# A two-layer trunk on one core: layer loops written out, an output stage of its own for the last layer, and 64 bytes more in one small tensor

## The reference, cut to what matters

```python
for l in range(2):
    h = h + 0.5 * swiglu(rmsnorm(h, ffn1_norm[l]), ffn1_w_in[l], ffn1_w_out[l])   # 1024 -> 2*2816 -> 1024
    u = rmsnorm(h, mix_norm[l]); parts = u @ w_in[l]
    y_a, y_b, y_c = sparse attention, pooling mixer, attention into 256 memory tokens
    h = h + (sum_i sigmoid(gate_i) * (y_i @ w_branch_i)) @ w_out[l]
    h = h + 0.5 * swiglu(rmsnorm(h, ffn2_norm[l]), ffn2_w_in[l], ffn2_w_out[l])
return rmsnorm(h, final_norm)        # x * rsqrt(mean(x*x) + 1e-6) * gain
```

## Time and profile before

| | |
|---|---|
| timed runs, median | 2253.84 us |
| profiled execution | 2246.63 us, span 2244.8 us |
| PE busy | 2216.6 us, 99% of the span |
| DVE, ACT, POOL busy | 42%, 23%, 59% |
| granted TensorE clock, mean | 0.997 of 2.4 GHz |
| chain that ended last | PE 93%, DVE 4%, issue, ACT, DMA 1% each |

### The profile page before, as it was taken

One profiled execution on the slowest core, in us unless ns is written; L12 is line 12 of the kernel. 1 busy time (PEld: TensorE's weight loads), 2 busy tenths in 40 slices (PEclk: granted clock), 3 DMA queues, 4 the chain that ended last, 5 costly groups with the idle time before them and its releaser, 6 DMA issues.

```text
span 2244.8 us, 31758 instructions
## 1 busy us (share of the span) xinstructions
PE 2216.6 (99%) x10262; PEld 1805.1 (80%) x10262; DVE 953.5 (42%) x1716; ACT 523.6 (23%) x1013; POOL 1325.7 (59%) x884
## 2 busy tenths in 40 slices
PE   9999999999999999999999999999999999999996
PEld 6888888877788888888888888888778888888885
DVE  5331344578855433023333223536877453321334
ACT  3110112443553210001111101125445432100111
POOL 7666657644436665665766566584444376656653
PEclk9999999999999999999999999999999999999998
DMA  5243223222113222332333332232211132223222
GB/s 183 96 134 107 94 80 118 93 69 68 62 54 107 94 94 86 101 103 76 105 102 121 110 107 94 76 130 78 69 62 66 48 121 95 93 83 105 99 79 76
DMA packets 68219, 209.88 MB, mean 93 GB/s; under 512 B 7536, under 2 KB 10776, under 8 KB 67864
## 3 DMA queue, kind: packets, MB, share of 16 engines
q1 hardware_dynamic: 64128, 203.62, 27.7%
q10 hardware_dynamic: 3992, 5.00, 0.7%
HBM read 206.48 MB, written 3.68 MB: 94 GB/s over the span
## 4 chain that ended last, share of the span: by engine, by line
PE 93%; DVE 4%; issue 1%; ACT 1%; DMA 1%; POOL 0%; DVEq 0%; ACTq 0%; POOLq 0%; SPq 0%
PE bank L608 29%; PE bank L607 28%; PE bank L606 28%; PE obank L859 1%; PE sbank L804 1%; PE tbank L826 1%; DVE picks L1356 1%; DVE top L1354 1%; PE obank L617 0%; PE sbank L796 0%; PE sbank L779 0%; DMA h<-in_xT 0%; PE obank L843 0%; PE sbank L757 0%; PE sbank L810 0%
## 5 line engine op out<-in xcount | busy, mean ns | idle before, releaser
L541 POOL TENSOR_TENSOR wL<-raw,wH 128x1024 fp32r<-128x1024 f32 (+3 forms) x424 | 896.0, 2113 | 35.4
L538 POOL TENSOR_SCALAR wH<-raw 128x1024 fp32r<-128x1024 f32 (+3 forms) x424 | 397.4, 937 | 842.1 <-PE bank L608 820.1
L608 PE MATMUL bank<-u0L,wH 128*128 128x512 f32 x1376 | 542.1, 394 | 0.0
L607 PE MATMUL bank<-u0H,wL 128*128 128x512 f32 x1376 | 539.3, 392 | 0.0
L606 PE MATMUL bank<-u0H,wH 128*128 128x512 f32 x1376 | 536.1, 390 | 0.0
L607 PEld LDWEIGHTS bank<-u0H,wL 128*128 128x128 f32 x1376 | 258.3, 188 | 61.1 <-issue 1.0
L606 PEld LDWEIGHTS bank<-u0H,wH 128*128 128x128 f32 x1376 | 258.3, 188 | 58.4 <-issue 1.0
L608 PEld LDWEIGHTS bank<-u0L,wH 128*128 128x128 f32 x1376 | 258.7, 188 | 51.5
L606 PE MATMUL bank<-u1H,wH 128*128 128x512 f32 x704 | 293.2, 416 | 0.0
L608 PE MATMUL bank<-hidL,wH 128*128 128x512 f32 x704 | 277.4, 394 | 0.0
L607 PE MATMUL bank<-hidH,wL 128*128 128x512 f32 x704 | 276.0, 392 | 0.0
(11 more groups left out here) (189 smaller groups left out, 2177.8 us busy)
## 6 DMA issues: line engine op xcount, KB each, us to landing
raw<-in_wA SPq DMA_DIRECT2D x176, 512.0 KB, 3.2
raw<-in_wM SPq DMA_DIRECT2D x96, 512.0 KB, 3.3
raw<-in_wB SPq DMA_DIRECT2D x64, 384.0 KB, 3.0
raw<-in_wB SPq DMA_DIRECT2D x64, 320.0 KB, 2.9
raw<-in_wR SPq DMA_DIRECT2D x32, 256.0 KB, 2.5
mem<-in_memT SPq DMA_DIRECT2D x2, 1024.0 KB, 6.9
near_bias<-bias_rows ACTq DMA_DIRECT2D x2, 1024.0 KB, 6.4
outT<-gate_a SPq DMA_DIRECT2D x4, 512.0 KB, 2.7
```

The lines of the kernel that those rows point to most:

```text
L538: pool.tensor_scalar(wH[:, w, 0:cols], raw[:, slot, 0:cols], 1.0, 0.0, ALU.mult, ALU.add).then_inc(rounded, 1)
L541: pool.tensor_tensor(wL[:, w, 0:cols], raw[:, slot, 0:cols], wH[:, w, 0:cols].bitcast(F32), ALU.subtract).then_inc(split_done, 1)
L607: pe.matmul(dst, b, hi[:, k, :], start=False, stop=False)
L608: mm = pe.matmul(dst, a, lo[:, k, :], start=False, stop=last and i == len(tiles) - 1)
```

## The change

There are four parts.

1. `for l in range(L)` takes the place of the loop over layers on PE, ACT and DVE (not on POOL and SP). Values of waits become constants there, except inside the loops over j.
2. The last layer has a last stage of its own. u0H, u0L and the copy to `h` are gone for it. DVE adds the residual in the bank, ACT squares out of the bank, and of blocks 0 to 3 ACT also writes bank times gain to `h`; blocks 4 to 7 stay in their banks. Seven squares are added up in `ssq`; the eighth goes to `ta`, and PE adds it by a second product into the same bank.
3. The output rows 4 to 7 are made by DVE out of the banks, rows 2 and 3 by DVE from `h`, rows 0 and 1 by POOL from `h`. Each row is its own transfer of 256 KB, six issued by SP and two by ACT.
4. `eps` has 48 floats in place of 32. All that is allocated after it moves by 64 bytes: `sg` to byte 128768 (1006 x 128), `u0H` to 133120 (1040 x 128), `u0L`, `hidH`, `hidL`, `yH`, `yL` likewise to a multiple of 128. Nothing ahead of it moves.

```diff
+LAST_BY_VECTOR = (4, 5, 6, 7, 2, 3)
+LAST_BY_POOL = (0, 1)
...
-        eps = sb("eps", [P, LINE // 4])
+        eps = sb("eps", [P, LINE // 4 + LINE // 8])
...
-            with pe.Fori(0, L) as l:
+            for l in range(L):
...
-            pe.wait_ge(ssq_added, L * 24 + 8)
-            mean_square(over_d[:, :], ssq, L * 5 + 1)
+            pe.wait_ge(norm_taken, L * 5 + 1)
+            pe.wait_ge(ssq_added, L * 24 + 7)
+            pe.matmul(obank[:, :], over_d[:, :], ssq[:, :], start=True, stop=False)
+            pe.wait_ge(squared, L * 24 + 8)
+            pe.matmul(obank[:, :], over_d[:, :], ta[:, :], start=False, stop=True).then_inc(norm_mean, 1)
...
+                    act.preload_act_table_set("natural_log_exp_and_others")
+                    for k in range(KD):
+                        act.wait_ge(h_added, l * 24 + (16 + k + 1))
+                        if k >= 2 and k < KD - 1:
+                            act.wait_ge(ssq_added, l * 24 + (24 + k - 1))
+                        act.activation(sbank[k % 2][:, :] if k < KD - 1 else ta[:, :], bank[k % BANKS][:, :],
+                                       ACT.Square).then_inc(squared, 1)
+                        if k < 4:
+                            act.activation(h[:, k, :], bank[k % BANKS][:, :], ACT.Copy,
+                                           scale=gain(G_NEXT, k)).then_inc(evacuated, 1)
...
+            for n, k in enumerate(LAST_BY_POOL):
+                act.wait_ge(out_ready_pool, n + 1)
+                act.dma_start(out[:, k, :], gate_a[:, k, :]).then_inc(out_stored[k], 16)
...
+            for k in range(KD):
+                total = bank[k % BANKS][:, :]
+                dve.wait_ge(unit_used, unit_at(L - 1, U_FFN2 + 60 + 2 * k + 1))
+                dve.scalar_tensor_tensor(total, total, 0.5, h[:, k, :], ALU.mult, ALU.add).then_inc(h_added, 1)
+                if k < KD - 1:
+                    dve.wait_ge(squared, L * 24 + (k + 1))
+                    dve.wait_ge(ssq_added, L * 24 + k)
+                    dve.tensor_tensor(ssq[:, :], sbank[k % 2][:, :], ssq[:, :], ALU.add).then_inc(ssq_added, 1)
             inverse_rms(L * 5 + 1, rms[:, :])
-            for k in range(KD):
-                dve.scalar_tensor_tensor(gate_a[:, k, :], h[:, k, :], gain(G_NEXT, k), rms[:, :],
-                                         ALU.mult, ALU.mult).then_inc(out_ready, 1)
+            for k in LAST_BY_VECTOR:
+                if k >= 4:
+                    dve.scalar_tensor_tensor(gate_a[:, k, :], bank[k % BANKS][:, :], gain(G_NEXT, k), rms[:, :],
+                                             ALU.mult, ALU.mult).then_inc(out_ready, 1)
+                else:
+                    dve.tensor_tensor(gate_a[:, k, :], h[:, k, :], rms[:, :], ALU.mult).then_inc(out_ready, 1)
```

More of the change, by code:

```diff
@@ L417, in trunk @@
         out_ready = sem("out_ready")
-        out_stored = [sem(f"out_stored{s}") for s in range(4)]
+        out_stored = [sem(f"out_stored{k}") for k in range(KD)]
+        out_ready_pool = sem("out_ready_pool")
         vector_step = sem("vector_step")
@@ L429, in apart @@
         def apart(eng, *waits):
-            waits = [(s, eng.to_reg(value)) for s, value in waits]
+            waits = [(s, value if isinstance(value, int) else eng.to_reg(value)) for s, value in waits]
             eng.wait_ge(gain_loaded, 16)
@@ L519, in _ @@
             layer(L - 1)
[L521 to L525, removed]
+            for n, k in enumerate(LAST_BY_VECTOR):
+                sp.wait_ge(out_ready, n + 1)
+                sp.dma_start(out[:, k, :], gate_a[:, k, :]).then_inc(out_stored[k], 16)
+            for k in LAST_BY_VECTOR:
+                sp.wait_ge(out_stored[k], 16)
         @block.gpsimd
@@ L583, in _ @@
                 ffn_units(U_FFN2)
+            pool.wait_ge(norm_taken, L * 5 + 2)
+            for k in LAST_BY_POOL:
+                pool.tensor_tensor(gate_a[:, k, :], h[:, k, :], rms[:, :], ALU.mult).then_inc(out_ready_pool, 1)
         @block.tensor
@@ L986, in _ @@
                           ).then_inc(bias_repeated, 16)
-            with act.Fori(0, L) as l:
+            for l in range(L):
                 def ffn(chunk, hid_from, root_n, hi, g, n_from):
@@ L1188, in _ @@
                 ffn(C_FFN2, sum(HALF), 5, u0H, G_NEXT, 24)
-                last_half(C_FFN2, 24, G_NEXT, u0H)
+                if l < L - 1:
+                    last_half(C_FFN2, 24, G_NEXT, u0H)
+                else:
[9 more added lines that the diff above has]
+                                           scale=gain(G_NEXT, k)).then_inc(evacuated, 1)
                 own.restart()
             root(L * 5 + 1, rms[:, :])
+            for n, k in enumerate(LAST_BY_POOL):
+                act.wait_ge(out_ready_pool, n + 1)
+                act.dma_start(out[:, k, :], gate_a[:, k, :]).then_inc(out_stored[k], 16)
+            for k in LAST_BY_POOL:
+                act.wait_ge(out_stored[k], 16)
         @block.vector
@@ L1240, in _ @@
             own.restart()
-            with dve.Fori(0, L) as l:
+            for l in range(L):
                 def ffn(unit, chunk, hid_from, norm_n):
@@ L1574, in _ @@
                 ffn(U_FFN2, C_FFN2, sum(HALF), 5)
-                last_half(U_FFN2, 24, G_NEXT, u0H, u0L)
-            inverse_rms(L * 5 + 1, rms[:, :])
-            for k in range(KD):
-                dve.scalar_tensor_tensor(gate_a[:, k, :], h[:, k, :], gain(G_NEXT, k), rms[:, :],
-                                         ALU.mult, ALU.mult).then_inc(out_ready, 1)
+                if l < L - 1:
+                    last_half(U_FFN2, 24, G_NEXT, u0H, u0L)
+            own.restart()
+            for k in range(KD):
[6 more added lines that the diff above has]
+                    dve.tensor_tensor(ssq[:, :], sbank[k % 2][:, :], ssq[:, :], ALU.add).then_inc(ssq_added, 1)
+            inverse_rms(L * 5 + 1, rms[:, :])
+            for k in LAST_BY_VECTOR:
+                if k >= 4:
+                    dve.scalar_tensor_tensor(gate_a[:, k, :], bank[k % BANKS][:, :], gain(G_NEXT, k), rms[:, :],
+                                             ALU.mult, ALU.mult).then_inc(out_ready, 1)
+                else:
+                    dve.tensor_tensor(gate_a[:, k, :], h[:, k, :], rms[:, :], ALU.mult).then_inc(out_ready, 1)
 def tiles(w):
```

## The result

The changed kernel takes 2258.73 us (median of 10 runs, 2257.98 to 2259.55). The kernel before took 2254.11 us beside it (10 runs, 2246.24 to 2255.05). The ratio is 1.0028, with an interval of 1.0018 to 1.0037: slower, where 2232 us was forecast with a range of 2221 to 2247. The profiled execution has a span of 2257.3 us against 2244.8, that is 12.5 us more.

The account below looks back on a forecast made before the run. PE, busy 99% of the span, was taken as the bound: number of matmuls times their distance, plus a tail. Gains of 14.4 + 0.7 + 1.5 + 4.9 = 21.5 us took 2253.84 to 2232 us, range 2221 to 2247.

Parts of the forecast that it names:

- The 64 bytes: Matmuls on u0, hid and y: moving them to multiples of 128 bytes saves 14.4 us, bounds 0 and 16.
- half of it: Rival: some streams, say hid and y, stay slow; 8.9 us gained in place of 14.4, time 2238; chance 0.07.
- The objection taken from the Trainium skill: Matmul distance: N / 2.4 GHz plus about 2.5 ns, no word on addresses; address gain 0, whole near 2246.
- Loops: Loops over layers written out on PE, ACT and DVE: 0.7 us between layers and 1.5 us in the mixing stage.
- boundary: End of layer 0 on PE: without the branch and its registers 0.7 us goes, bounds 0 and 0.75.
- mixing: Mixing stage: fewer register instructions ahead of waits on DVE, ACT and PE gain 1.5 us, bounds -1 and 7.
- the 7.0 us named: Mixing stage: PE's seven short waits for ACT and DVE, 7.0 us, of which a fifth was taken as gain.
- The tail: After the last product: 4.3 us gained up to Ln and 0.65 in the output rows, 4.9 us together.
- the shared port: Output rows: DVE's rows 2 and 3 would wait 0.2 us for POOL, hidden by the transfers.
- Code fetched late: Rival: PE's program written twice makes some 50 code reads cost 0.75 us each, 37 us, time 2269; chance 0.03.
- the 7.2 us between that profile and the median: Whole kernel: profiled execution 7.2 us below the timed median; forecast 2225.1 for the profiled execution, 2232 for timed runs.
- the better bounds: Range's lower end: 2221 from all terms at their better bounds and the level of the profiled execution.

Follow-up runs that it names:

- e2: Kernel before with only eps enlarged from 32 to 48 floats: 2270.89 us, ratio 1.0094 to the kernel before.
- e1: Changed kernel with eps back at 32 floats, so u0, hid and y at their old addresses: 2238.20 us, ratio 0.9943 to the kernel before.
- e7: Kernel before with only eps at 80 floats, putting u0, hid and y at the weights' remainder modulo 256 bytes: 2232.54 us, ratio 0.9914.
- e3: Changed kernel with eps at 80 floats, u0 at byte 133248: 2221.04 us, ratio 0.9872 to the kernel before.
- m2: PE-only loop, not the kernel: weights and moving operand shifted in 32-byte steps, also fewer columns; 226.7 to 234.6 ns per 512-column matmul.
- m1: PE-only loop, not the kernel: 512-column moving operand shifted in three rooms of SBUF; 227.0 to 233.3 ns per matmul with weights at remainder 128.
- e5: Kernel before with only the loops over layers of PE, ACT and DVE written out: 2243.07 us, ratio 0.9954.
- e6: Kernel before with only DVE's loop over layers written out: 2243.66 us, ratio 0.9958.

## Why the prediction was wrong, step by step

**The 64 bytes: wrong in sign, and this alone decided.** The step that failed is the reading "What sets u1 apart is where it lies: at a multiple of 128 bytes, while y, u0 and hid start 64 bytes off." From it came the term of 14.4 us gained; the runs show 23.2 us lost in its place, because u0, hid and y went from difference 64 to difference 128. The trace had two values of one thing, and three descriptions fit them: the place in SBUF, the alignment, and the distance to the weights. The prediction weighed the first two and never worked out the third; its rival *half of it* says only that "more than the moving operand counts". In the kernel before the weights have remainder 128 modulo 256, u1 also 128 (difference 0, 226.7 ns) and u0 192 (difference 64, 228.8). The change set u0 to remainder 0, which is difference 128, the slow class. The working from blocks to time was sound: 2208 blocks at +0.0105 give 23.2 us. e2 shows it on the kernel before (24.4 us between spans), and e1 on the changed one (2257.3 - 2236.6 = 20.7, and 3.7 more for e1's slow half). The 14.4 us forecast from 0.0065 came out as 13.5 where the address was put right (e7). The term's bounds were 0 and 16; nothing in the trace excluded a loss, and the term needed one.

The objection taken from the Trainium skill, "TensorE: Matmul & The Clock Gate", section "Wait — 56ns, not 53.3ns?", is not borne out either: by it the term was to be 0, and a fixed cost on top of N / 2.4 GHz leaves no room for 226.7, 228.8 and 233 ns at one N. No run here has matmuls without a weight load before each, so none tests the formula where no weights are loaded.

**Loops: boundary right in number, mixing too small.** Between the two profiles the boundary gave 0.75 us for 0.7. That was in part luck: the same branch, in other executions and kernels, cost 0.15 to 0.9 us over the 0.23 of the written-out form, so "the branch with the registers behind it" isn't one price. In the mixing stage 1.5 us were taken of 7.0, "because these waits end with instructions of 0.4 to 0.7 us and not with registers"; it was 6.6, inside the bounds. Of the 7.0 us named, the 3.9 for `sg` went and 2.7 to 2.8 for `picks` stayed; 0.9 came from `probs`, and some 1.4 stand in no wait that the profile lists. The releaser's own duration says nothing of how late it was started: the registers stood one engine farther back, on DVE, before the work that ACT waited for.

**The tail: right.** Ln came 2.68 us after the last product (2.8 forecast), behind the second table load, which ends at 2245.73, just before Ln; the second product takes 1.13 us, not 2.07. PE idled 0.56 us ahead of it, and the granted clock is 1.00 of full speed from 2244.4 to 2245.7 us; before, PE idled 4.89 us ahead of L617, and it is 0.50 from 2230.3 to 2232.5. Output bytes run at about 400 GB/s and end some 6.8 us after the first row starts (7.0). In all 4.8 to 5.1 us gained in e1, e3 and after, 4.9 forecast. POOL's two rows took 2.48 us and ended at 2251.91, before DVE came to its two rows from SBUF at 2252.09. So the 0.2 us that the prediction expected from the shared port didn't arise, and this run can't show whether it would.

**Code fetched late: did not happen.** The chance of 0.03 for slower was given to this rival, and it wasn't what made the kernel slower: the second layer starts 0.23 us behind the first, and the blocks of u1 keep 0.680 us.

**From span to median: a second miss.** Profile against profile the changes are +23.2 - 0.75 - 6.6 - 5.1 = +10.8 us, and measured 12.5. Of the rest 1.2 us lie in the start of the kernel (the first full block on u0 starts at 26.09 in place of 24.91 us) and 0.5 in the products on y with 256 columns (118.4 ns in place of 113.3). The medians are only 4.6 us apart, since the median of before, 7.5 us above its profiled execution, lies by its time among executions with two slow halves, and the changed kernel showed no second rhythm. The prediction took the 7.2 us between that profile and the median as an offset that any version would keep. It was a property of difference 64. The lower end of the range, 2221, doesn't follow from what is said of it: the better bounds add up to 29.2 us (16 + 0.75 + 7 + 5.4), which is 2224.7 from the median and 2217.5 from the profiled execution.

## What to carry to other kernels

Where two groups of equal matmuls stand at different distances, list the addresses of both operands, of weights too, before naming a cause, and ask which rules fit both values and what each predicts for the new place; if they disagree in sign, the range must show it. On this chip the start of the moving operand minus that of the weights should be 0 modulo 256 bytes for matmuls of 512 fp32r columns: here that is one number in one `sb` call, and it takes the changed kernel from 2258.7 to 2221.0 us, below both kernels. With 256 columns difference 0 was the slowest in m2, so the column count has to be looked at too. A wait is shortened at the head of its chain, which needn't be the engine that the profile names. And before two kernels are compared, see whether their profiled and timed executions run in the same rhythm.

## What the runs showed of the hardware

- Distance of 512-column fp32r matmuls, each with a weight load, by (moving - weights) modulo 256 bytes: 226.7 to 227.7 ns at 0, 228.8 to 230.0 at 64, 232 to 235 elsewhere (m1, m2). No dependence at 128 columns, and difference 0 the slowest at 256 (119.8 ns, m2). The place in SBUF has no effect (m1, e3).
- At difference 64 two stable rhythms, 228.9 and 233.3 ns, entered at the start of a half of a feed-forward part and kept to its end (before, e1, e5, e6). The three profiled executions of before, with no, one and two slow halves, lie in the three groups of its timed runs.
- Loading a table that is already loaded costs ACT the full 1.28 us: in the changed kernel L1203 loads it at 2190.16, L961 again at 2244.45, and nothing else is loaded between.
- Transfers of 256 KB in 2048-byte pieces leave as fast as those of 512 KB in 4096-byte pieces, about 400 GB/s (after and before, the last 6 us).
